# Attention score tiles of a head taken in the order 7, 6, sample, 3, 5, 4, 2, 1, 0

## The reference, cut to what matters

```
sc = einsum(q, k) * SCALE (+ forgetting term in layer 1)
sc = where(key is not ahead of the query, sc, NEG)
pr = softmax(sc, axis=-1)
o  = einsum(pr, v)
```

## Time and profile before

| | us |
|---|---|
| median of three runs | 3100.68 (3099.67 to 3102.58) |
| the profiled execution's own time | 3105.76 |
| its span, first to last instruction | 3104.0 |
| TensorE busy (share of the span) | 2945.3 (95%) |
| VectorE busy | 2039.2 (66%) |
| ScalarE busy | 1253.8 (40%) |
| GpSimd busy | 1629.5 (52%) |

### The profile page before, as it was taken

The page is one execution under the profiler, slowest core; times in us unless marked ns, Lnnn a source line. Parts: engine busy times, 40 slices in busy tenths (PEclk is TensorE's granted clock), DMA queues, the critical chain, the costliest instruction groups (busy, mean ns, idle before and its releaser), DMA issues.

```text
span 3104.0 us, 55804 instructions
## 1 busy us (share of the span) xinstructions
PE 2945.3 (95%) x18498; PEld 2838.8 (91%) x18498; DVE 2039.2 (66%) x3917; ACT 1253.8 (40%) x2663; POOL 1629.5 (52%) x1243
## 2 busy tenths in 40 slices
PE   7999999998999999998989999999899999999987
PEld 7889999988999999998988988889799999999887
DVE  4656888556666666667664589964766666666765
ACT  4234777435222222224442177752522222232452
POOL 4223555467555555555554455554855555554553
PEclk9999999998999999998989999999899999999998
DMA  3497554221111111113102575631211111111301
GB/s 115 154 326 245 135 145 127 90 94 53 48 41 54 47 41 54 47 48 125 42 21 105 172 176 136 153 84 61 92 42 54 47 41 58 43 48 54 126 34 56
DMA packets 175613, 281.94 MB, mean 91 GB/s; under 512 B 95248, under 2 KB 121376, under 8 KB 175120
## 3 DMA queue, kind: packets, MB, share of 16 engines
q1 hardware_dynamic: 175504, 280.51, 28.5%
HBM read 206.39 MB, written 74.07 MB: 90 GB/s over the span
## 4 chain that ended last, share of the span: by engine, by line
PE 63%; issue 14%; POOL 12%; DVE 7%; ACT 2%; DMA 1%; POOLq 0%; SPq 0%; DVEq 0%; ACTq 0%
PE ps L1531 27%; PE ps L1181 11%; PE ps L1183 11%; PE ps L1182 11%; POOL probs L1006 8%; DVE sublayer_out L2366 1%; PE ps L1471 1%; DVE act_lo L2381 1%; PE ps L1202 1%; POOL pre_sums L964 1%; PE ps L1216 1%; DVE pre_sums L2342 1%; DVE post_sums L2342 1%; POOL weight_hi L928 1%; DVE stage_lo L2465 1%
## 5 line engine op out<-in xcount | busy, mean ns | idle before, releaser
L2611 DVE TENSOR_TENSOR sublayer_out<-ps,sublayer_out 128x352 f32<-128x352 f32 x1008 | 527.0, 523 | 481.8 <-PE ps L1183 478.7
L1181 PE MATMUL ps<-act_hi,weight_hi 128*128 128x352 f32 (+2 forms) x1392 | 473.0, 340 | 30.3 <-DVE weight_lo L2410 10.9
L1006 POOL TENSOR_TENSOR probs<-probs,row_inv 128x1024 f32<-128x1024 f32 (+8 forms) x288 | 311.8, 1092 | 295.1 <-DVE row_inv L2543 294.8
L1182 PE MATMUL ps<-act_lo,weight_hi 128*128 128x352 f32 (+2 forms) x1392 | 459.9, 330 | 0.0
L1183 PE MATMUL ps<-act_hi,weight_lo 128*128 128x352 f32 (+2 forms) x1392 | 459.8, 330 | 0.0
L1531 PE MATMUL ps<-act_hi,weight_lo 128*128 128x352 f32 x1280 | 413.8, 323 | 0.0
L1531 PE MATMUL ps<-act_hi,weight_hi 128*128 128x352 f32 x1280 | 413.3, 323 | 0.0
L1531 PE MATMUL ps<-act_lo,weight_hi 128*128 128x352 f32 x1280 | 413.0, 323 | 0.0
L942 POOL TENSOR_TENSOR weight_lo<-weight_raw,weight_hi 128x1024 fp32r<-128x1024 f32 x113 | 278.9, 2468 | 224.8 <-ACT weight_hi L1940 208.0
L1084 POOL TENSOR_TENSOR weight_lo<-weight_raw,weight_hi 128x512 fp32r<-128x512 f32 x160 | 205.1, 1293 | 248.4 <-ACT weight_hi L2023 248.4
L1181 PEld LDWEIGHTS ps<-act_hi,weight_hi 128*128 128x128 f32 (+2 forms) x1392 | 268.7, 193 | 38.6 <-issue 22.8
(11 more groups left out here) (217 smaller groups left out, 7615.2 us busy)
## 6 DMA issues: line engine op xcount, KB each, us to landing
weight_raw<-units SPq DMA_DIRECT2D x201, 512.0 KB, 3.6
k_hi<-kB_hi SPq DMA_DIRECT2D x32, 328.0 KB
qA_hi<-stage_hi SPq DMA_DIRECT2D x16, 528.0 KB, 3.7
qA_lo<-stage_lo SPq DMA_DIRECT2D x16, 528.0 KB, 4.7
q_hi<-qA_hi SPq DMA_DIRECT2D x16, 528.0 KB
q_lo<-qA_lo SPq DMA_DIRECT2D x16, 528.0 KB
residual_kept<-residual SPq DMA_DIRECT2D x6, 1408.0 KB, 8.6
residual<-residual_kept SPq DMA_DIRECT2D x6, 1408.0 KB, 10.1
```

The source lines that it names most:

```text
L1006: pool.tensor_tensor(p, p, rinv[0:M, k:k + 1].to_broadcast((M, KEYS[tile])), ALU.mult).then_inc(at_p, 1)
L1181: nc.tensor.matmul(out, ah, bh, start=first, stop=False)
L1182: nc.tensor.matmul(out, ah, bl, start=False, stop=False)
L2611: V.tensor_tensor(y[:, m, c], src, y[:, m, c], ALU.add).then_inc(f_acc, 1)
```

## The change

The fourth tile of a head is now 3 in place of 0, and the last three are 2, 1, 0 in place of 1, 2, 3. The PSUM banks go with the steps, not with the tiles, so the pattern of banks is as before. In the list of turns tiles 2 and 3 (four blocks and three) now come first, as chunks 8 and 9, and tiles 0 and 1 are chunk 10. The output part of tiles 0 to 3 ends with chunk 10 as before.

```
-ORDER = [7, 6, 8, 0, 5, 4, 1, 2, 3]
+ORDER = [7, 6, 8, 3, 5, 4, 2, 1, 0]
-RUNS = [(6, 7), (8,), (4, 5), (0, 1), (2, 3)]
+RUNS = [(6, 7), (8,), (4, 5), (2, 3), (0, 1)]
-S_BANK = {7: 0, 6: 2, 8: 0, 0: 1, 5: 2, 4: 0, 1: 2, 2: 3, 3: 2}
+S_BANK = {7: 0, 6: 2, 8: 0, 3: 1, 5: 2, 4: 0, 2: 2, 1: 3, 0: 2}
-OUT_AFTER = {8: 0, 4: 1, 3: 2}
+OUT_AFTER = {8: 0, 4: 1, 0: 2}
 ...
-    if run == (0, 1):
+    if run == (2, 3):
         return 3 * hp + PART_OF[8] + 1
 ...
-                    if first and layer and tile == 0 and s < STEPS:
+                    if first and layer and tile == 3 and s < STEPS:
                         stored()
```

## The result

The changed kernel takes 3113.84 us (median of 6 runs, 3110.62 to 3116.22), the kernel before on the same chip 3100.18 us. The ratio is 1.0044, 95% interval [1.0034, 1.0054]: slower by 10.5 to 16.7 us. In a second series it was 3112.19 against 3099.04, ratio 1.0035 [1.0023, 1.0048]. The forecast was 3113.6, in a range of 3103 to 3119. It was built on a median of 3100.68 for the kernel before, so it said +12.9 us where +13.7 was measured.

The account below looks back on a forecast made before the run. Bound: a chain closing once a head through chunk 9's turn, ScalarE and VectorE, with TensorE nearly full in layer 0. Layer 0 7.1, layer 1 6.0, start 0.7, drain -0.9 sum to +12.9: 3113.6 us, range 3103 to 3119.

Parts of the forecast that it names:

- (b): Behind chunk 9's turn: three blocks shorten the copies, VectorE's output instruction starts 1.10 after the high part, not 1.35; 0.25 back.
- (a): ScalarE: tile 3's exp waits for chunk 9's turn, so chunk 9's high part starts 0.72 us after the turn's end.
- (c): TensorE's longer fourth-step scores and later chunk 2 products: up to 0.24 + 0.13 in layer 1, 0.35 + 0.03 in layer 0.
- The slack I had read: Layer 0, first head: chunk 2's low part ends at 404.48, products start at 404.73; 0.13 later low part moves them +0.03.
- (d): Next head's second step, layer 1: tile 6's scores no longer wait for tile 3's exp; -0.26 us once a pair.
- the drain: End of each layer: (b) holds without (a), and tile 0's short maximum precedes the last turns; -0.45 a layer, -0.9.
- Only the chain counts: First rival: TensorE's fourth-step columns are saved at the ninth, so (c) is 0; 6.6 less 0.2, 3107.1; chance 0.18.
- Gain by the maximum moved away: Second rival: 0.41 us of VectorE maximum a head moves into idle time, shortening seventh-step waits; 3089.5; chance 0.08.
- Cancelling: Third rival: (d) and shorter waits in layer 1 pay for (a) in layer 0; within 5 us of 3100.7; chance 0.07.
- Worse by a few tenths a head: Fourth rival, first form: each wait worsens VectorE's and TensorE's later meetings; 3122; chance 0.07 shared with the clock form.
- Worse by the clock: Fourth rival, second form: TensorE granted 0.9 clock in layer 1, 29 us over the layer; 3143; chance 0.07 shared.

Follow-up runs that it names:

- exp_behind: Changed kernel with ScalarE's exp of the fourth step issued behind chunk 9's high part and the output part; 3097.94 us, ratio 0.9996 to the kernel before.
- after_long9: Changed kernel with tile 0's scores, in the ninth step, made over 512 keys instead of 128, the extra columns unused; 3106.80 us, one run.
- order_120: Changed kernel with tiles 1 and 2 exchanged, so the last three tiles are 1, 2, 0; 3112.53 us, one run.
- before_behind: Kernel before with the exp of the fourth step (tile 0) issued behind chunk 9's high part and the output parts; 3100.48 us, ratio 1.0001.
- before_long4: Kernel before with tile 0's scores, in the fourth step, made over 512 keys instead of 128, the extra columns unused; 3108.05 us, one run.
- behind_120: exp_behind with the last three tiles in the order 1, 2, 0; 3095.47 us, ratio 0.9991 to the kernel before.
- behind_012: exp_behind with the last three tiles in the order 0, 1, 2; 3093.01 us, ratio 0.9980 to the kernel before.
- before_both: Kernel before with the edits of before_wait9 and before_long4 together; 3108.88 us, one run.
- before_wait9: Kernel before with the exp of tile 0 at the fourth step made to wait for the turn of chunk 9; 3109.28 us, one run.

## Why the prediction was right

The number was right, and the runs show the mechanism in the main; one path of the forecast, that of (b), was another than it said. The signs that it named came out: the exp of tile 3 starts 0.04 us after the turn of chunk 9 (forecast within 0.1), the high part follows it without idle time, TensorE's waits for an exp in layer 1 are 13.6 / 7 = 1.9 us a pair (forecast 2.1) and there are 13 of them in seven pairs of layer 0 (forecast two a pair), and the pairs are 37.1 and 35.2 (forecast 37.1 and 35.4). What was off are sizes in layer 1 and at both ends of attention.

**The chain (a).** In first heads of layer 1 the high part starts 1.21 after the turn's start, forecast 0.55 + 0.72 = 1.27. The exp from start to next start took 1918.34 - 1917.66 = 0.68. By the rule of the Trainium skill (Perfetto Trace Analysis, "Optimizing Scalar/DVE Operations") it would have been nearer 0.6. The page speaks of the fixed overhead of an instruction, which the profile shows about twice because the write-acknowledgement half overlaps with the next instruction, and not of half its whole length, as my sentence can be read. In this case the copy behind the exp overlaps by about 0.1 us, 0.48 long with its next start after 0.37, and the exp, which is followed by the read of its sum, by nothing. The row decided rightly. The turn was the term off: 0.49 and not 0.55. exp_behind took the term away and got 11.0 us.

**The shorter chain (b).** 1.10 instead of 1.35 in first heads, as forecast, but by another path, so the exact match is luck. I had added the high part, ScalarE's copy of the output and 0.05. What VectorE's output instruction follows is its own low part: 0.48 + 0.03 for the high part, 0.56 for the low part, 0.03 to the next start. It was so before as well (1914.11 + 0.69 = 1914.80 for the low part, the output instruction at 1914.83, ScalarE's copy done at 1914.57). Only in second heads does ScalarE's copy come last now: it starts 0.50 after the high part (1936.17 - 1935.67) and not 0.37, and from the high part to TensorE's scores there are 4.00 instead of 4.12, where first heads have 3.86 instead of 4.11. The same delay of the second head can be read in the kernel before, 1931.37 - 1930.75 = 0.62 instead of 0.50, hidden there behind the longer low part:

```profile
1931.37 0.59 ACT L1909 ACTIVATE act_hi<-ps 64x512 f32 x1
1931.38 0.69 DVE L2548 TENSOR_TENSOR probs_t_lo<-ps,probs_t_hi 128x512 fp32r<-128x512 f32 x1 [0.81 <-ACT probs_t_hi L1902]
...
1932.11 0.69 DVE L2558 TENSOR_TENSOR out_partial<-ps,act_hi 64x512 f32<-64x512 f32 x1
```

Why the copy starts later in second heads isn't shown: its row names no releaser.

**TensorE (c).** The fourth step took 0.53 instead of 0.28 in layer 1, forecast +0.24. The products of chunk 2 came 0.12 to 0.13 later after each resumption, forecast +0.13, and waited in layer 1 as forecast. That the ninth step's saving is lost, after_long9 shows. For layer 0 I had put the later products at +0.03 in first heads and 0 in second ones. From TensorE's resumption at the seventh step to the turn of the sample's chunk it takes 5.11 instead of 5.07 us behind a first head and 5.48 instead of 5.43 behind a second, so +0.04 and +0.05. The slack I had read was there: with the short scores and the short maximum together (order_120) the same stretch takes 4.97 and 5.35, so the low part could come about 0.1 later than before at no cost, and 0.04 to 0.05 is what is left of 0.13. The 0.13 a head of order_120 is against the changed kernel, where that slack has been used up.

**The tile-6 wait (d).** It went, with 0.33 in first heads of layer 1, forecast 0.26. In second heads I had none; there, too, a gap of about 0.1 us ahead of these scores closed.

By heads (time from one resumption at the seventh step to the next, against before): layer 0 +0.62 and +0.29, forecast 0.67 and 0.25; layer 1 +0.36 and +0.20, forecast 0.51 and 0.27. In layer 1, first head, the missing 0.15 are 0.07 of (d), 0.06 of the turn and 0.02 of the block that the turn of chunk 8 has more. In the second, 0.07 is missing: 0.09 of (d), 0.06 of the turn and 0.05 of that block, less the 0.13 that (b) did not give.

**The sum.** From the first turn of the sample's chunk to the last, layer 0 grew by 7.07 (forecast 7.1) and layer 1 by 4.75 (6.0). Behind the last one attention ended 1.06 and 1.24 sooner, where I had 0.45 each: the drain was under-counted by 1.4. At the start (first scores to the first turn of the sample's chunk), layer 0 was 1.5 shorter and layer 1 1.5 longer, where I had 0.7 in all. The first is an accident of the profile of before: TensorE was granted half its clock (0.50) for some 3 us there, and before_behind, with the same order, has 13.88 to the first such turn instead of 15.16, beside 13.66 of after. The profile of before_long4 has such a stretch too, and 15.05. Without that stretch attention grew by about 10.8, in the interval of the two series (7 to 17). So +12.9 was 2 us too much by attention, and the median was met to 0.2 us partly by luck.

**The rivals.** Only the chain counts: refuted by before_long4 (+5 of attention with the exp untouched) and by after_long9. (Its sum used 0.44 for layer 1 where its own terms give 0.47, which would have made it 0.2 us more.) Gain by the maximum moved away: VectorE's lateness does matter, 0.13 a head for every 128 columns of maximum at the seventh step (order_120, behind_120, behind_012), but the change makes that maximum longer, and its exp did wait for the turn. Cancelling: layer 1 loses as well. Worse by a few tenths a head: both pairs came out at the forecast or below. Worse by the clock: inside the pairs it stayed at 1.00 with 2.8 us idle a pair in layer 1. The swing that the Trainium skill tells of (TensorE: Matmul & The Clock Gate, "A second HAM failure mode: psum-queue depth-cycling") didn't come.

## What to carry to other kernels

When a table sets the order of work, look at what each entry does to the in-order lists of the other engines: here a tile that merely exchanged places became one that waits for the latest turn, and everything queued behind it on ScalarE stood in the chain that closes once a head. Before an order is given up, try to issue the newly waiting instruction one place later; that one line was worth 11 us of attention. Time saved ahead of a wait for another engine is not saved, and the place to save it is the engine that is waited for: here the maximum that precedes the last low part. And compare the members of the chain one by one, not only their sum: here I took one instruction for the last link that was another, and the sum didn't show it.

## What was not expected of the hardware

TensorE's clock at the start of layer 1's attention. By the windows of one microsecond it was granted 0.50 (1.2 GHz) in both kernels at first; before it rose in the window that begins 11.0 us after the first scores, after in the one that begins 15.0 after them:

```profile
1797.96:1798.96 1.00, 1.00 (x7) 0.67 (x6) 1.00 (x3) 0.93 (x3) 0.90 (x1) 0.72 1.00 212
```

```profile
1795.67:1796.67 1.00, 0.82 (x3) 0.62 (x3) 0.66 (x1) 0.44 (x2) 1.00 (x2) 0.50 0.99 205
...
1801.67:1802.67 1.00, 1.00 (x7) 1.00 (x6) 0.64 (x2) 0.41 (x1) 0.34 (x1) 0.50 1.07 170
1802.67:1803.67 1.00, 1.00 (x11) 1.00 (x10) 0.57 (x3) 0.50 (x2) 0.35 (x1) 0.96 0.02 3
```

The first is of before, the others are of after, where TensorE had been idle for 0.18 us some 8 us behind its first scores. Before, it was busy in every window from 6 us behind them on. The first sample's turn came after 16.67 us instead of 15.15. exp_behind has 16.63 and before_behind 15.20, so it looks like a price of the order, paid once. after_long9 speaks against that: it has the order of after and the same pause of 0.18 us, 8.5 us behind its first scores, but its clock rose in the window that begins 12.0 us behind them, and its first sample's turn came after 15.97:

```profile
1799.37:1800.37 1.00, 1.00 (x9) 0.78 (x7) 1.00 (x3) 0.94 (x3) 0.73 (x1) 0.88 0.96 208
```

The kernels with the order of before lie between 14.76 (before_both) and 15.82 (before_wait9). So neither the order nor that pause settles it alone, and the cause stays open. In pairs, pauses of up to 1.04 us left the clock at 1.00.
